# Attention stage: a second buffer of probabilities, and another order of four steps on the engines

## The reference

```python
q, k, v = attn_project(x, w_qkv)              # 16 query heads, 4 key/value heads, head size 64
q, k = rope(q, pos), rope(k, pos)             # rotary positions
s = einsum('...qkgd,...skd->...kgqs', qg, k) * HEAD_DIM ** -0.5
s = where(0 <= qpos - kpos <= 128, s, -inf)   # a window of 128 keys before each query
m = maximum(max(s), sink); p = exp(s - m)     # one sink value per head
w = p / (sum(p) + exp(sink - m))
o = einsum('...kgqs,...skd->...qkgd', w, v)   # then o @ w_o, residual, layer norm
```

## Time and profile before

| | |
|---|---|
| median of three runs | 2918.62 us |
| profiled execution, its own time | 2922.73 us |
| its span (first to last instruction) | 2920.9 us |
| PE busy, share of the span | 97% |
| DVE, ACT, POOL busy | 51%, 31%, 20% |
| PE's share of the chain that ended last | 87% |
| mean granted clock of PE | 0.985 of full speed |
| the four attention groups | 12.0 to about 416 us |

### The profile page before, as it was taken

One profiled execution on the slowest core, in us unless ns is written; L12 is line 12 of the kernel. 1 busy time (PEld: TensorE's weight loads), 2 busy tenths in 40 slices (PEclk: granted clock), 3 DMA queues, 4 the chain that ended last, 5 costly groups with the idle time before them and its releaser, 6 DMA issues.

```text
span 2920.9 us, 44283 instructions
## 1 busy us (share of the span) xinstructions
PE 2837.8 (97%) x18132; PEld 2730.7 (93%) x18132; DVE 1484.0 (51%) x2974; ACT 902.4 (31%) x1686; POOL 597.3 (20%) x505
## 2 busy tenths in 40 slices
PE   7999989999999999999999999899999999999997
PEld 6888869999999999899999999899899999999996
DVE  5555576544444444613445354365675444444446
ACT  5344445222211112422343433432252221222213
POOL 2333351000000002402223232122231000000004
PEclk9999989999999999999999999999999999999998
DMA  4210111111111112134566565766401111111101
GB/s 131 77 31 16 44 32 48 54 44 44 44 47 55 44 44 64 55 121 135 178 199 187 182 196 180 231 220 211 143 30 58 58 44 44 46 57 44 44 25 58
DMA packets 193433, 260.49 MB, mean 89 GB/s; under 512 B 29200, under 2 KB 151696, under 8 KB 193200
## 3 DMA queue, kind: packets, MB, share of 16 engines
q1 hardware_dynamic: 128336, 196.16, 21.7%
q10 hardware_dynamic: 64896, 61.50, 6.1%
HBM read 191.50 MB, written 68.20 MB: 89 GB/s over the span
## 4 chain that ended last, share of the span: by engine, by line
PE 87%; DVE 5%; issue 3%; ACT 2%; POOL 2%; DMA 1%; SPq 0%; DVEq 0%; POOLq 0%; ACTq 0%
PE bank L493 28%; PE bank L495 27%; PE bank L494 27%; POOL a_prob L2067 1%; PE bank L638 1%; ACT y L1023 1%; PE bank L546 1%; PE bank L932 1%; PE bank L628 1%; DVE xl L1507 1%; DVE y L1480 1%; PE bank L895 0%; PE bank L880 0%; POOL a_qk L2056 0%; DVE bank L1492 0%
## 5 line engine op out<-in xcount | busy, mean ns | idle before, releaser
L493 PE MATMUL bank<-xh,wh 128*128 128x344 f32 x3624 | 1171.7, 323 | 12.6 <-DMA xl<-scratch_heads_lo 8.0
L495 PE MATMUL bank<-xh,wl 128*128 128x344 f32 x3624 | 1160.2, 320 | 0.0
L494 PE MATMUL bank<-xl,wh 128*128 128x344 f32 x3624 | 1159.9, 320 | 0.0
L493 PEld LDWEIGHTS bank<-xh,wh 128*128 128x128 f32 x3624 | 684.0, 189 | 28.7 <-issue 18.4
L494 PEld LDWEIGHTS bank<-xl,wh 128*128 128x128 f32 x3624 | 683.5, 189 | 5.3 <-issue 0.7
L495 PEld LDWEIGHTS bank<-xh,wl 128*128 128x128 f32 x3624 | 683.7, 189 | 0.0
L1470 DVE TENSOR_TENSOR y<-bank,y 128x344 f32<-128x344 f32 x576 | 289.8, 513 | 225.0 <-PE bank L495 224.5
L2115 POOL TENSOR_TENSOR f_hl<-f_cv,f_hh 128x344 fp32r<-128x344 f32 x132 | 123.1, 933 | 1268.2 <-ACT f_hh L1171 1268.2
L493 PE MATMUL bank<-f_hh,wh 128*128 128x344 f32 x1056 | 339.8, 322 | 0.0
L495 PE MATMUL bank<-f_hh,wl 128*128 128x344 f32 x1056 | 337.4, 319 | 0.0
L494 PE MATMUL bank<-f_hl,wh 128*128 128x344 f32 x1056 | 337.1, 319 | 0.0
(11 more groups left out here) (234 smaller groups left out, 3492.4 us busy)
## 6 DMA issues: line engine op xcount, KB each, us to landing
raw<-in_w SPq DMA_DIRECT2D x216, 512.0 KB, 3.7
scratch_qkvg<-p_plain ACTq DMA_DIRECT2D x96, 172.0 KB, 2.9
r_s<-in_state_in SPq DMA_DIRECT2D x32, 512.0 KB, 3.7
out_state_s<-r_s ACTq DMA_DIRECT2D x32, 512.0 KB, 5.6
scratch_qkvg<-p_rot ACTq DMA_DIRECT2D x24, 344.0 KB, 2.9
xh<-scratch_heads_hi SPq DMA_DIRECT2D x12, 688.0 KB, 8.6
xl<-scratch_heads_lo SPq DMA_DIRECT2D x12, 688.0 KB, 9.6
r_cxq<-scratch_qkvg SPq DMA_DIRECT2D x32, 256.0 KB, 5.6
```

What stands on the lines that cost most here:

```text
L493: pe.matmul(out, ah, bh, start=(k == 0), stop=False)
L494: pe.matmul(out, ah, bl, start=False, stop=False)
L495: mm = pe.matmul(out, al, bh, start=False, stop=(k == n - 1))
```

## The change

`a_prob` becomes two buffers, used in turn (`b % 2`); the 4 KB per partition come out of an unused gap, so that every tile behind the gap keeps its place. `exps(b)` now waits for `turn_probs(b - 2)`, and newly for `inverse(b - 1)`, as the row sums still have one buffer. In a round of the loop PE does `scores(t-2)` right behind `project(t)`; ACT does `exps(t-2)` ahead of `pt_in(t-3)`; DVE does `shift(t-2)` ahead of `t_lo(t-1)`. The next group's `project(0)` and `project(1)` and its `scores(0)` wait only for the last add of the group before that reads the PSUM bank which they overwrite (adds 20, 21, and 22 and 23). The list behind the loop is unchanged.

```diff
-        K.a_prob = sb("a_prob", [P, GH, 2 * W])
+        K.a_prob = sb("a_prob", [P, 2, GH, 2 * W])
...
-        sb("a_gap", [P, 2176])
+        sb("a_gap", [P, 1152])
...
+        def freed(g, b):
+
+            q = max(q for q in range(24) if att_bank(g - 1, q) == b)
+            name, value = EV["ao", g - 1, q]
+            return S[name], value
...
             if b == 0:
                 wait_slab(pe, S, 5 * g + 2)
-                after(pe, S["yadd"], 24 * g)
+            if b < 2 and g:
+                pe.wait_ge(*freed(g, b))
...
         def scores(b):
+            if b == 0 and g:
+                pe.wait_ge(*freed(g, 3))
+                pe.wait_ge(*freed(g, 4))
...
-                    mm = pe.transpose(bank[5 + t][:, h * W:(h + 1) * W], K.a_prob[:, h, t * W:(t + 1) * W], ident[:, :])
+                    mm = pe.transpose(bank[5 + t][:, h * W:(h + 1) * W], K.a_prob[:, b % 2, h, t * W:(t + 1) * W], ident[:, :])
...
         for t in range(NB + 1):
             project(t)
+            if t >= 2:
+                scores(t - 2)
             if t >= 1:
                 turn(t - 1)
             if t >= 4:
                 values(t - 4)
-            if t >= 2:
-                scores(t - 2)
             if t >= 3:
                 turn_probs(t - 3)
...
-            after(act, T["pt"], NB * g + b)
+            after(act, T["pt"], NB * g + b - 1)
+            after(act, T["inv"], NB * g + b)
...
                 heads_hi(t - 4)
+            if t >= 2:
+                exps(t - 2)
             if t >= 3:
                 pt_in(t - 3)
-            if t >= 2:
-                exps(t - 2)
...
             rope(t)
+            if t >= 2:
+                shift(t - 2)
             if t >= 1:
                 t_lo(t - 1)
...
-            if t >= 2:
-                shift(t - 2)
             if t >= 4:
                 heads_lo(t - 4)
```

More of the change, by code:

```diff
@@ L1082, in exps @@
             k0 = 0 if b else W
-            after(act, T["pt"], NB * g + b)
+            after(act, T["pt"], NB * g + b - 1)
+            after(act, T["inv"], NB * g + b)
             for h in range(GH):
-                act.activation(K.a_prob[:, h, k0:], K.a_sm[:, h, k0:], ACT.Exp, bias=K.a_st[:, 2, h:h + 1],
+                act.activation(K.a_prob[:, b % 2, h, k0:], K.a_sm[:, h, k0:], ACT.Exp, bias=K.a_st[:, 2, h:h + 1],
                                accum_out=K.a_st[:, 4, h:h + 1])
@@ L2066, in probs @@
             k0 = 0 if b else W
-            pool.tensor_tensor(K.a_prob[:, :, k0:], K.a_prob[:, :, k0:],
+            pool.tensor_tensor(K.a_prob[:, b % 2, :, k0:], K.a_prob[:, b % 2, :, k0:],
                                K.a_st[:, 7, :].rearrange("p (h a) -> p h a", a=1).to_broadcast([P, GH, 2 * W - k0]),
```

## The result

The changed kernel takes 2904.01 us (median of five runs, 2901.50 to 2907.15), the kernel before 2920.1 us in five runs beside it (2915.71 to 2921.79). The ratio is 0.9949, with a 95% interval from 0.9939 to 0.9960: some 15 us faster (12 to 18). The forecast had been 18.6 us, just outside that interval, and 2900 us, inside its own range of 2892 to 2911. The profiled execution took 2901.5 us, with a span of 2899.7 us.

What follows compares the result with a forecast made beforehand. PE bounds the kernel, busy 2837.8 of 2920.9 us, so only its waits or lower-clock work can be won. Terms 7.7 + 6.3 + 2.3 + 1.05 + 1.3 = 18.6 us off the 2918.6 us median gave 2900 us, range 2892 to 2911.

Steps and rivals of the forecast that it cites:

- Loop waits: In the attention groups' rounds, PE's waits for POOL's `probs` would go: 7.7 us, bounds 0 to 7.7.
- End of the group: Behind each group's loop, an earlier samples' turn and add 0 would start `values(5)` 1.6 us sooner: 6.3 us over four groups.
- Between groups: A new group's projection would start at once, 0.75 us earlier, three times: 2.3 us, bounds 0 to 2.5.
- Group 0: Rounds 2 and 3: scores fill 1.05 us of the `add_rope` wait, and PE's clock stays at 2.4 GHz, 1.3 us.
- rival B: Low clock behind the sample tokens' scores moves: bad side 4 us lost, 2904 us, chance 0.08; good side 2895.5 us.
- a mean clock below 0.985: Sign of rival B: PE's granted clock lower than 0.985 although the waits are gone.
- A: Group's end gives its gain back, as `values(5)` starts no earlier relative to DVE's adds: 12.3 us won, 2906 us, chance 0.12.
- C: New PE wait at `values` for `pt_in`, now behind `exps` on ACT: slower, 2936 us if 3.3 us late; chance 0.05.
- D: Idle time moves elsewhere in the round, so only the starts of groups are won: 2916 us, chance 0.09.
- the faster cases: Forecast (0.66), A (0.12) and rival B's bad side (0.08), all faster by over 0.2%; the prediction gave faster 0.87.
- groups 1 to 3 each 3.9 us shorter: Sign that the forecast is right, in attention groups 1 to 3; group 0 was to be some 6 to 7 us shorter.

Runs made afterwards that it cites:

- one_buffer: Changed kernel with all its orders but a single probabilities buffer, so exponentials wait for the turned probabilities of the block before; 2902.8 us, ratio 0.9944.
- pe_dve_order: Kernel before with only the new PE order (scores right behind the projection) and DVE order (`shift` ahead of `t_lo`); 2906.2 us, ratio 0.9957.
- turn_first: Changed kernel, but in each round PE does the turn ahead of the scores; 2904.9 us, ratio 0.9950.
- freed_only: Kernel before with only the narrower waits between the groups; 2914.4 us, ratio 0.9983.
- samples_split: Changed kernel with the sample tokens' scores in two halves of four, output projection jobs 6 and 7 between them; 2899.1 us, ratio 0.9937.
- split_end: Changed kernel with samples_split's halves, and at each group's end DVE's last `shift` and add 4 ahead of `heads_lo(NB - 3)`; 2900.7 us, ratio 0.9935.
- best: split_end with PE's turn ahead of the scores, except in each group's last round and round 2 of group 0; 2898.5 us, ratio 0.9931.

## Why the prediction was right, and where its sum was off

**Loop waits, 7.7 us: all gone.** The chain of side engines has the lengths that the rows of before gave, and starts 2.4 to 2.6 us earlier. What brings it forward is `shift` ahead of `t_lo` with the scores early enough for it. The prediction gave ACT's order and the buffer a share; one_buffer and pe_dve_order show that they have none. This part of its mechanism was wrong, and the number hides it.

**The term that was missing: PE's own order, 3.0 us.** The prediction priced the move of the scores on PE at nothing. A round without a wait went from 7.49 to 7.64 us and from 8.07 to 8.22, in rounds 4 to 8 of four groups, 20 x 0.15. turn_first gives back 0.15 in each of rounds 5 to 7 without touching anything else; in round 4 it gives 0.07, as the wait of that round had been priced 0.08 us too high. Behind a projection the turn's first matmul started 4.31 us after the projection's; the scores' starts after 4.39. And the turn, with scores before it, holds PE for 0.47 us instead of 0.42. Why a step costs more behind another one no run here shows.

**End of the group, 6.3 us forecast.** From the samples' turn of group 1 to the first projection of group 2, 37.73 us became 35.68: 2.05 us, where 1.29 + 0.75 had been worked out. `down(0,4)` gave 1.17 of it, and the next group's start 0.86. Before the turn, the loop of group 1 shrank by 1.29 us: forecast 1.63 + 0.29, less the 0.75 of PE's order is 1.17.

**Between groups, 2.3 us.** As forecast in kind, alone (freed_only) and in the whole; in size it is 0.93 us a start and not 0.75, so 2.8.

**Group 0.** The wait at the turn went from 1.8 to 1.0 us and the clock stayed at 2.4 GHz behind it, as forecast (2.3 us). That the shorter wait kept the clock up is not shown: in turn_first the wait is 1.7 us, and the clock stayed up as well. The forecast had not seen that the first projections would run at the lower level for longer in this execution: from the start of the first to the first turn 11.1 us instead of 10.4.

**Clock, rival B.** Its mechanism was real and took 1.5 us of the forecast, in group 2. The sign that the prediction named for it, a mean clock below 0.985, did not show: the mean was 0.990, as other stages had more of the high level. samples_split ties the low level to the run of tiny matmuls. Rivals A, C and D did not come: no wait of job 2, none of `values` for `a_pt` in any round. (The chances given for the faster cases add up to 0.86, not 0.87.)

**Groups.** The sign "groups 1 to 3 each 3.9 us shorter" did not come: group 1 lost 3.3 and group 2, with its clock, 2.0. Group 0 lost 6.15, as forecast.

**Sum.** 18.6 - 3.0 (order on PE) - 1.5 (group 2's clock) - 0.7 (start) = 13.4 us for attention, against 15.5 in the traces. Of the difference of 2.1 us 0.5 lies in the starts of the groups and 0.5 in a first projection that starts 0.5 us earlier. 1.0 lies behind the last loop of group 3, where before two stretches of 10.2 and 6.8 us at the lower clock stood and now two of 3.4. I have no experiment for that place, nor for the clock in retention and the last FFN. The medians, 16.1 us apart, agree with the attention stage within their spread. So that the time came within 4 us of the forecast is in part luck: a term that was left out and two of the clock were met by gains that nobody had forecast.

## What to carry to other kernels

When a chain over several engines is late, look for the instruction that stands ahead of it in a strict list and waits for something the chain doesn't need: here the rests of the turned queries on DVE. Moving it made a second buffer superfluous, once PE's scores came early enough to pay for it at the end of a group; so try the order first, and count PE's steps again after a move, as the same matmuls in another order took 2% longer. And look at what a stretch of tiny matmuls does to the clock behind it, even where PE is never idle.

## What the runs showed of the hardware

- PE can fall to the 1.2 GHz level behind work without an idle gap: behind 16 matmuls of 4 columns (1.94 us) the next 3.4 us ran at a granted clock of 0.50 in the changed kernel, and the level follows them in 19 of 36 groups in the nine profiles that have them in a row. With the same 16 split in two groups of 8, and 12 matmuls of 344 columns between them, the clock stayed at 1.00 behind them in all four groups, in three kernels (samples_split, split_end, best). A group with the low level took 98.48 us, one without 97.11, in the same execution of the kernel before.
- A step of PE costs up to 0.1 us more or less by what stands before it: transposes follow a projection at 4.31 us from its start, matmuls over 64 rows at 4.39.
- A GpSimd add beside the row maxima of VectorE (one input in PSUM, one in SBUF) kept its time (0.73 us at 151.87 in the changed kernel), while beside a split with two inputs in SBUF it took 2.57 us instead of 0.45.
